# Token scales moved from the norm's input to the projections' results, and the stage boundaries of a 16-stage network re-ordered

## The reference, cut to what matters

```
norm 0 -> stick-breaking attention     norm 1 -> MLP (squared relu, 4096 hidden)
norm 2 -> retention                    norm 3 -> MLP
norm 4 = final norm of the first network, its result is the new h
norm 5 -> gated linear attention (GLA) norm 6 -> conv FFN (2816 x 2 hidden, 3 taps over tokens, silu gate)
norm 7 -> shared keys and values of NSA;  norm "7b": the same h and root, another gain -> NSA's queries
norm 8 -> conv FFN                     norm 9 -> output
rms_norm(x, g) = x * rsqrt(mean(x*x) + 1e-6) * g        one factor for each token (rstd), one gain for each column
```

## Time and profile before

| what | value |
|---|---|
| times of three runs | 1498.61, 1498.81, 1499.96 us; median 1498.81 |
| span of the profiled execution | 1498.3 us, 0.5 below the median of the runs |
| TensorE busy | 1402.6 us (94%) |
| VectorE, ScalarE, POOL busy | 829.9 (55%), 728.0 (49%), 254.1 us (17%) |
| chain that ended last | TensorE 82%, VectorE 7%, ScalarE 5%, waits for nothing shown 3%, POOL 2% |
| mean granted TensorE clock | 0.980 |
| memory read | 229 MB, 154 GB/s over the span |

### The profile page before, as it was taken

The page is one execution under the profiler, slowest core; times in us unless marked ns, Lnnn a source line. Parts: engine busy times, 40 slices in busy tenths (PEclk is TensorE's granted clock), DMA queues, the critical chain, the costliest instruction groups (busy, mean ns, idle before and its releaser), DMA issues.

```text
span 1498.3 us, 21802 instructions
## 1 busy us (share of the span) xinstructions
PE 1402.6 (94%) x8780; PEld 1241.0 (83%) x8780; DVE 829.9 (55%) x897; ACT 728.0 (49%) x896; POOL 254.1 (17%) x219
## 2 busy tenths in 40 slices
PE   6977999999999899999999889999989887999997
PEld 6956889988987688989887869999988665799996
DVE  4443655556544546555457646665656765465664
ACT  5476544444344335444447435555555465355553
POOL 0011000002500000000001303333302234043332
PEclk9999999999999999999999999999999989999999
DMA  8520555554554244555533145555544302255551
GB/s 310 174 108 1 183 193 194 192 177 164 174 193 163 90 169 157 196 196 172 193 129 138 56 146 182 183 193 184 180 137 147 111 1 84 95 187 181 185 196 56
DMA packets 32616, 231.12 MB, mean 154 GB/s; under 512 B 3616, under 2 KB 3616, under 8 KB 5408
## 3 DMA queue, kind: packets, MB, share of 16 engines
q1 hardware_dynamic: 31104, 224.41, 43.1%
q10 hardware_dynamic: 1440, 5.68, 1.0%
HBM read 229.02 MB, written 1.05 MB: 154 GB/s over the span
## 4 chain that ended last, share of the span: by engine, by line
PE 82%; DVE 7%; ACT 5%; issue 3%; POOL 2%; DMA 0%; ACTq 0%; POOLq 0%; DVEq 0%
PE ps L509 25%; PE ps L510 25%; PE ps L511 25%; DVE w_lo L1283 1%; POOL arena L468 1%; PE ps L721 1%; DVE h L1338 1%; PE ps L865 1%; ACT w_hi L939 1%; PE ps L872 1%; ACT x_hi L953 1%; ACT L1052 1%; DVE x_lo L1295 1%; POOL arena L438 1%; PE ps L495 0%
## 5 line engine op out<-in xcount | busy, mean ns | idle before, releaser
L1283 DVE TENSOR_TENSOR w_lo<-ring,w_hi 128x2048 fp32r<-128x2048 f32 x212 | 486.3, 2297 | 363.8 <-ACT w_hi L939 363.4
L939 ACT ACTIVATE w_hi<-ring 128x2048 fp32r<-128x2048 f32 x212 | 404.5, 1909 | 237.7 <-PE ps L511 236.3
L509 PE MATMUL ps<-x_hi,w_hi 128*128 128x256 f32 x1664 | 475.1, 285 | 10.2 <-DVE x_lo L1295 10.2
L510 PE MATMUL ps<-x_lo,w_hi 128*128 128x256 f32 x1664 | 474.4, 285 | 0.0
L511 PE MATMUL ps<-x_hi,w_lo 128*128 128x256 f32 x1664 | 474.3, 285 | 0.0
L509 PEld LDWEIGHTS ps<-x_hi,w_hi 128*128 128x128 f32 x1664 | 322.7, 194 | 13.1 <-issue 8.9
L510 PEld LDWEIGHTS ps<-x_lo,w_hi 128*128 128x128 f32 x1664 | 322.5, 194 | 1.2
L511 PEld LDWEIGHTS ps<-x_hi,w_lo 128*128 128x128 f32 x1664 | 322.8, 194 | 0.0
L509 PE MATMUL ps<-w_hi,y_hi 128*128 128x512 f32 (+1 forms) x624 | 244.1, 391 | 14.4 <-issue 6.2
L510 PE MATMUL ps<-w_lo,y_hi 128*128 128x512 f32 (+1 forms) x624 | 241.6, 387 | 0.0
L511 PE MATMUL ps<-w_hi,y_lo 128*128 128x512 f32 (+1 forms) x624 | 241.1, 386 | 0.0
(11 more groups left out here) (197 smaller groups left out, 1293.4 us busy)
## 6 DMA issues: line engine op xcount, KB each, us to landing
ring<-ws SPq DMA_DIRECT2D x212, 1024.0 KB, 4.9
tab<-tables ACTq DMA_DIRECT2D x4, 550.0 KB, 3.6
rowg<-rows ACTq DMA_DIRECT2D x3, 512.0 KB, 4.5
h<-x SPq DMA_DIRECT2D x2, 512.0 KB, 5.7
out<-arena SPq DMA_DIRECT2D x2, 512.0 KB, 2.6
arena<-decay ACTq DMA_DIRECT2D x1, 768.0 KB, 5.1
sm<-small ACTq DMA_DIRECT2D x1, 742.0 KB, 5.6
arena<-narrow ACTq DMA_DIRECT2D x1, 296.0 KB, 5.7
```

Source lines behind the costliest of these rows:

```text
L509: mm(o, lh, rh, start=start, stop=False, skip_group_check=True)
L510: mm(o, lh, rl, start=False, stop=False, skip_group_check=True)
L939: A(w_hi[:, s, :], ring[:, s, :], ACT.Copy).then_inc(hi_ready, 1)
L1283: V.tensor_tensor(w_lo[:, s, :], ring[:, s, :], w_hi[:, s, :].bitcast(F32), ALU.subtract).then_inc(lo_ready, 1)
```

## The change

The token factor leaves the path in front of the projections.

- **Turning over.** The unscaled `h` is transposed (`turn_over`), a token tile at a time, and `x_hi`/`x_lo` are made in tiles of 128 x 128. `keep_clock` at boundaries goes.
- **Ordering by token tile.** `close` runs the last one or two pieces of a stage for the first token tile, then for the second, with the transposes of the first tile between the second tile's matmuls.
- **Values first.** Before retention, GLA and NSA the two pieces of a `natural` projection now come first; they begin with the first token tile, and the second tile is turned over after three of their matmul groups.
- **The factor.** `fold` makes it later. Values and gates take it as ScalarE's `scale` when they are evacuated. Queries and keys take it as a product with `scale`, a 128 x 256 tile with the token factor in each row, on VectorE (`scaled`). That tile comes from two fp32 matmuls of `ones` with a diagonal (`spread`, norms 0, 2, 5 to 8). Retention's cosine and sine tables are multiplied by it. The MLPs take `1 / mean square` in the residual. In GLA `rstd4 * rstd5` is used, and the final gain is folded into norm 5's.
- **Conv FFN.** VectorE first copies each unit out of PSUM times `scale` into `conv_in`; the taps then read `conv_in` in SBUF.
- **Slots.** `ring` has 2 slots, `w_hi`/`w_lo` have 4, `y_hi`/`y_lo` 8 rows instead of 12, and up to four banks turn.

The core of the diff:

```diff
-RING = 3
+RAW = 2
+RING = 4
@@ SyncE
-                if turn is not None or g >= RING:
-                    sp.wait_ge(lo_ready, plus(g - RING + 1, turn, RING))
+                if turn is not None or g >= RAW:
+                    sp.wait_ge(lo_ready, plus(g - RAW + 1, turn, RAW))
@@ TensorE
+            def turn_over(n, t):
+                for k in range(KT):
+                    if n == 0:
+                        pe.wait_ge(x_loaded[t], 16)
+                    elif n != "7b" and k % 4 == 0:
+                        pe.wait_ge(h_ready, H_AT[4 if n == 5 else n] - 3 + 2 * t + k // 4)
+                    if t == 1 and k % 2 == 0 and n != 0:
+                        pe.wait_ge(xT_lo, 8 * XT_OF[n] + k // 2 + 1)
+                    r = nc.tensor.transpose(ps[:, 4 + k // 2, t * T + (k % 2) * P:t * T + (k % 2 + 1) * P],
+                                            h[:, t, k * P:(k + 1) * P], ident)
+            def spread(n):
+                pe.wait_ge(diag_ready, SCALE_OF[n] + 1)
+                for t in range(TT):
+                    r = mm(ps[:, 2, t * P:(t + 1) * P], ones[:, :], diag[:, t, :], start=True, stop=True, ...)
+            def close(pieces, n):
+                for t in range(TT):
+                    for i, (g, tiles) in enumerate(pieces):
+                        end = i == len(pieces) - 1
+                        for k in range(2):
+                            r = add(g, tiles, t, k, False, end)
+                            if n is not None and t == 1 and end and k == 0 and len(pieces) == 1:
+                                turn_over(n, 0)
+                        if t == 0 and end:
+                            r.then_inc(half_done, 1)
+                        if t == 1:
+                            r.then_inc(done, 1)
+                            if n is not None and not end:
+                                turn_over(n, 0)
@@ hidden.up
+                        if u == 0 and n in SCALE_OF:
+                            spread(n)
@@ NSA on TensorE
-            norm(7)
+            natural(G_NSA, (0, 1), first=7)
+            spread(7)
             for u in range(4):
-                transposed(G_NSA + u, u, nsa_freed, first=7 if u == 0 else None)
-            natural(G_NSA + 4, 4, nsa_freed)
-            pe.wait_ge(nsa_freed, 6)
-            norm("7b")
+                transposed(G_NSA + 2 + u, 4 + u)
+            for t in range(TT):
+                pe.wait_ge(nsa_kv, 4)
+                turn_over("7b", t)
@@ ScalarE
+            def norm(n, *late):
+                tiles(n, 0)
+                tiles(n, 1)
+                for g in late[:-1]:
+                    refill(g)
+                sumsq(4 if n == 5 else n)
+                refill(late[-1])
@@ ScalarE, GLA's tree
             for j in range(8):
-                if j % 2 == 0:
+                if j in (0, 2, 4):
...
                 A(w, w, ACT.Exp, scale=-1.0 / 16.0).then_inc(gla_decay, 1)
                 if j < 4:
-                    refill(G_GLA + 5 + j)
+                    refill(G_GLA + 6 + j)
@@ ScalarE, NSA
             for u in range(2):
-                act.wait_ge(done, G_NSA + u + 1)
+                act.wait_ge(nsa_kv, u + 1)
...
-                refill(G_NSA + u)
+                refill(G_NSA + 2 + u)
             for u in range(2, 4):
-                evac(u, G_NSA + u, ns_k[:, u - 2, :, :], nsa_freed)
-                refill(G_NSA + u)
...
+                refill(G_NSA + 2 + u)
             for t in range(TT):
-                evac(4 + t, G_NSA + 5, ns_v[:, t, :], nsa_freed)
-            norm_tiles("7b")
-            refill(G_NSA + 5)
+                tiles("7b", t)
@@ VectorE
+            def scaled(dst, src, sc, by=1.0):
+                return V.scalar_tensor_tensor(dst, src.rearrange("p (a t) -> p a t", t=T), by,
+                                              sc.unsqueeze(1).broadcast_to([P, 2, T]), ALU.mult, ALU.mult)
@@ VectorE, residual
+                        if n in (2, 4):
+                            r = V.scalar_tensor_tensor(v, ps[:, 2 * t + c, :], rfold[:, t:t + 1], v, ALU.mult, ALU.add)
+                        else:
+                            r = V.tensor_tensor(v, ps[:, 2 * t + c, :], v, ALU.add)
+                        r.then_inc(h_ready, 1)
+                    if following is not None:
+                        tiles(following, t)
@@ VectorE, ffn
+                        dve.wait_ge(done, plus(g + 1, turn, st.each))
+                        scaled(conv_in[:, u % 2, :, :], ps[:, bank(u), :], scale).then_inc(freed, 1)
+                        dve.wait_ge(freed, plus(u + 1, turn, st.units))
+                        dve.wait_ge(base, plus(u + 1, turn, st.units))
                         for e in range(2):
                             v = conv[:, u % 2, e, 1:T]
-                            V.scalar_tensor_tensor(v, ps[:, bank(u), e * T:(e + 1) * T - 1], par(u, 2 + e, turn), v,
+                            V.scalar_tensor_tensor(v, conv_in[:, u % 2, e, 0:T - 1], par(u, 2 + e, turn), v,
                                                    ALU.mult, ALU.add).then_inc(tap, 1)
@@ VectorE, NSA
+            for u in range(4):
+                dve.wait_ge(done, G_NSA + 2 + u + 1)
+                scaled(ns_kvs[:, u, :, :] if u < 2 else ns_k[:, u - 2, :, :], ps[:, 4 + u, :], scale).then_inc(nsa_kv, 1)
+                refill(G_NSA + 2 + u)
+            for t in range(TT):
+                tiles("7b", t)
```

More of the change, by code:

```diff
@@ L511, in mm3, with transposed @@
                 return mm(o, ll, rh, start=False, stop=stop, skip_group_check=True)
[L513 removed]
+            def transposed(g, b, first=None, turn=None, each=0):
                 split(g, turn, each)
[L516 to L517 removed]
                 s = g % RING
@@ new lines, in hidden @@
+            def hidden(n, st, freed, ready, following):
+                def up(c, turn):
+                    for u in (2 * c, 2 * c + 1):
+                        if turn is not None or u >= 6:
+                            pe.wait_ge(freed, plus(u - 3, turn, st.units))
+                        transposed(st.up(c) + u % 2, bank(u), first=n if u == 0 else None, turn=turn, each=st.each)
+                        if u == 0 and n in SCALE_OF:
+                            spread(n)
+                def down(c, turn):
+                    pe.wait_ge(ready, plus(2 * c + 2, turn, st.units))
+                    if c == 0 and n in SCALE_OF:
+                        pe.wait_ge(scale_ready, SCALE_OF[n] + 1)
+                    pieces = [(st.down(c) + i, (4 * (c % 2) + 2 * i, 4 * (c % 2) + 2 * i + 1)) for i in range(st.dn)]
+                    if c == st.chunks - 1:
+                        close(pieces, following)
+                    else:
+                        for i, (g, tiles) in enumerate(pieces):
+                            accumulate(g, tiles, c == 0 and i == 0, turn, st.each)
@@ L1191, in _ @@
+            for u in range(4):
+                refill(G_NSA + 6 + u)
+                if u == 0:
                     for i in range(2):
@@ L1254, in _ @@
                     .then_inc(nsa_oT_hi, 1)
-            for i in range(3):
+            for i in range(2):
                 refill(G_NSA + 14 + i)
-            norm(8, G_NSA + 17)
+            norm(8, G_NSA + 16, G_NSA + 17)
+            spread(8, scale)
             ffn(1)
@@ L1584, in _ @@
                  .then_inc(nsa_blocks, 1)
-            for g in range(7, 10):
-                refill(G_NSA + g)
+            for u in range(4):
+                dve.wait_ge(done, G_NSA + 6 + u + 1)
+                scaled(ns_q[:, 2 * u:2 * u + 2, :], ps[:, 4 + u, :], scale, 0.125).then_inc(nsa_q_in, 1)
+                refill(G_NSA + 6 + u)
             dve.wait_ge(nsa_blocks, 2)
```

682 lines of the change are left out of this document (397 added, 285 removed).

## The result

The changed kernel takes 1504.73 us (median of 8 runs, 1501.84 to 1507.45), the kernel before 1499.53 us in the same sets (8 runs, 1498.61 to 1500.82). The ratio is 1.0032 with a 95% interval of 1.0023 to 1.0042: slower by 0.3%, where 1.1% faster was forecast. The profiled execution is the slowest of the eight (1507.45 us, span 1505.6), 2.7 above the median, so the spans differ by 7.4 us where the medians differ by 5.2: some 2 us of what the profiles show belong to this one execution.

A forecast was written before the change was run, and what follows sets the result against it. TensorE, busy 94% of the 1498.3 us span, was taken as the bound, so only its waits could be won. Terms 5.1 + 3.95 + 1.5 + 2.55 + 7.4 - 2.4 - 1.7 = 16.4 gave 1482.5 us, range 1471 to 1496.

The forecast's parts named there:

- the one on the conv FFNs: Conv FFN chunks: VectorE-ScalarE cycle of 16.8 to 16.95 us against TensorE's 16.95, no mid-stage stall; -1.7 us (0 to -10).
- Rival B: Conv FFNs: VectorE becomes the bound, cycle 17.3 us, 7 to 14 us lost, 1489 to 1497 us; chance 15%.
- rival C: Conv FFNs: taps, now reading only SBUF, wait for POOL's `y_lo`; 32 us delay less cover, 1511 us, slower; chance 8%.
- My sign of a wrong prediction: Conv FFNs: the prediction is wrong if, among other signs, the taps' mean is over 0.4 us.
- the 1.20 us in front of the first scores: NSA: of the 1.20 us the first scores waited for VectorE, 1.1 was to go.
- the term "0": Kernel start: first matmul 0.5 us earlier, spread costs 0.55; net 0 (-1 to 1).
- The 0.5 around the span: Whole kernel: 0.5 us between the 1498.3 us span and the 1498.8 us median, added to the forecast span.
- the wait of the spread for the diagonal: Conv FFN starts (boundaries 6 and 8): spread behind the first unit waits for the diagonal; 1.25 us given back each.
- "7b": Norm inside NSA: tiles stand behind the next refill in both queues; stall 11.5 us instead of 4.7, -6.8.
- the clock I had booked half: Boundaries 3, 6 and 8: slow stretches costing 5.1 us may vanish; half, 2.55 us, taken (0 to 5.1).
- Rival D: All boundaries: without warming matmuls the clock falls at every one, five more slow stretches at 1.7 us; 1491 us; chance 8%.
- Rival A: NSA: the queue in front of "7b" does not bite, the -6.8 and -1.7 are gone; 1474 us; chance 15%.

The follow-up runs named there:

- e1: Changed kernel without VectorE's scaled copy in the conv FFNs; ScalarE's base and VectorE's taps read PSUM as before, token factor left out of the hidden units: 1486.48 us.
- e6: Changed kernel with the conv FFN's scaled copy made twice, the first into a buffer nobody reads: 1525.47 us.
- e2: Changed kernel, same instructions, with a weight remainder on VectorE between a conv FFN unit's scaled copy and its taps: 1488.35 us, ratio to before 0.9924.
- e9: Changed kernel with e2's order in the conv FFNs and e4's NSA order and start warming, GLA as the change left it: 1477.96 us, ratio 0.9855.
- e10: As e9, with the conv FFN's product of silu and value made by VectorE behind the taps for every unit: 1478.14 us, ratio 0.9857.
- e5: The kernel before the change with no warming matmuls at its boundaries, nothing else: 1504.3 us, one run.
- e4: Changed kernel: NSA splits before raw copies, 7b tiles before last refill; GLA's last gates and ScalarE refill behind the tree; six warming products at the start: 1502.45 us.
- e7: Changed kernel with e2's, e4's and e8's GLA orders; last chunk's up refills behind taps, last unit's product on VectorE: 1488.01 us, ratio 0.9921.
- e8: Changed kernel with GLA's refill moved on both ScalarE and VectorE, and in NSA only norm 7b's tiles before the last refill: 1508.7 us.

## Why the prediction was wrong

**The step that failed** is the one on the conv FFNs: "the handing back and forth with ScalarE closes a cycle that I put at 16.8 to 16.95". It is 17.7, measured, and its price 8.7 and 9.2 us more than forecast, 17.9 of 23.8. Rival B (15%) had the cycle as the mechanism, with 17.3 and 7 to 14 us in all; the real figure is beyond its end, so the range ended too early. B's own sum, 21 times 0.35, is 7.4 us before the cover, and the 14 at its upper end has no working; 21 times the measured 0.77 is 16. Nor is VectorE full, as B's title has it (busy 65.6 of 102 us). I summed what each engine does and added a guess for the hand-offs, in place of walking one chunk instruction by instruction. From start to start in the rows above: copy, base and first unit's taps 4.0 (974.61 to 978.59), remainder 2.2, copy, base and second unit's taps 4.2 (980.79 to 984.95), silu 0.6, product *at its held price, which the earlier trace rows showed*, 2.3 (the second remainder runs beside it), `y_hi` 0.3, `w_hi` 1.9, remainder 2.2: 17.7. e1, e6 and e2 show the copy and its place in the order as the cause. I also placed the danger of VectorE and POOL holding one another wrongly: rival C had the taps wait for `y_lo`, but in the changed kernel they average 481 ns against 478 in e1; what is held is POOL's product, and it was held before too (mean 2295 ns), when TensorE set the pace. My sign of a wrong prediction, a mean of the taps over 0.4 us, says nothing: it was 478 ns before the change already.

**Mis-sized in the rest:** at NSA the head came as forecast (47.2 for 47.0 up to the small projection). From there to the first score it is 49.0 us where it was 47.2: I had let 1.1 of the 1.20 us in front of the first scores go, and 4.4 stand there now (row L961 above). From the first score to the stage's end it is 112.8 us where it was 107.7; tile 0's transposes are 1.1 of that, and about 4 are the scores, whose code is not changed. Windows of 108 us from the first score on, and the first 2 us of them, before and after:

```profile
1187.00:1295.00 108.00, 92.57 (x531) 70.19 (x532) 59.46 (x117) 54.88 (x163) 32.27 (x32) 0.94 0.15 49
...
1187.00:1189.00 2.00, 1.55 (x8) 1.12 (x8) 0.29 (x1) 0.56 (x1) 0.00 (x0) 1.00 0.02 8
```

```profile
1182.00:1290.00 108.00, 93.52 (x512) 69.90 (x513) 59.25 (x116) 54.96 (x162) 32.23 (x32) 0.88 0.13 43
...
1182.00:1184.00 2.00, 1.64 (x6) 1.49 (x7) 0.21 (x1) 0.74 (x1) 0.00 (x0) 0.50 0.19 70
```

The mean granted clock (last but two in a row) is 0.94 and 0.88 in the same work: 2 x 0.06 x 108 = 13 and 2 x 0.12 x 108 = 26 us at the lower level of 1.2 GHz. Part of it is chance of the execution: e9 and e10 have the same NSA code and 0.88 and 0.94 here, with NSA at 201.8 and 198.0. But part goes with the change. The two traces with the NSA of the kernel before (before, e5) wait 1.2 us in front of the first score and run it at full clock, with 0.94 and 0.95 in the 108 us; all ten traces on the changed kernel wait 4.1 to 4.6 us there and start the scores at half clock, for 3.4 to 10.2 us, and six of the ten have 0.88. That the longer wait is what brings the slow stretch is not shown, since no run shortened it; so how much of the 4 us the change costs stays open. At the start the term "0" was +2.1: TensorE's first matmul comes at 16.15 instead of 15.16. ScalarE now loads a table (1.28 us) and writes four `x_hi` in front of the first `w_hi`, which starts at 11.84 instead of 9.99, and the first remainder at 13.80 instead of 11.94. The slow stretch behind it, which was there before too, is 20 matmuls long instead of some 14; it varies from run to run. The 0.5 around the span was wrong as well: it compared the span of one execution with the median of others, while every run on record lies 1.7 to 2.3 above its own span.

**Right:** the boundaries (2.83 for 3.05), retention, GLA (copies 85.8 us behind the close, forecast 86.3), the wait of the spread for the diagonal (0.97 for 1.25), "7b" (11.8 for 11.5). Of the clock I had booked half; all three stretches were saved, where half was a guess and the better end luck. Rival D is false: no boundary fell. Rival A did not come by itself, but e4 shows what it took: 8.6 us up to the first score, where A has 8.5. My remark that an earlier evacuation would give GLA 2 to 6 us is untested: e4, e7 and e8 moved the last evacuation later, behind the tree.

## What to carry to other kernels

If a second engine no longer reads a result itself but a first engine's copy of it, it waits for the first engine's queue from then on. Walk one whole period through all queues, with hand-offs and held durations, and compare it with the bound to a per cent, since 4% over ten chunks shows only at the end of the stage. An engine with a third of idle time can be the bound by order alone; move independent work into the wait before adding buffers or moving work. A refill that is moved on one engine must be moved on all, and with few slots it takes its transfer with it.

## What was not expected of the hardware

The clock did not fall behind gaps of 2.8 us that hold transposes, with no warming in them (boundaries 1, 3, 6 and 8). In the kernel before it fell behind four boundaries of seven, all 6.7 us long and with warming matmuls in them, and not behind boundary 5, 11.0 us long with 6.17 us of warming; in e5, without any, it fell behind five of seven and still not behind boundary 5, where TensorE had 7.0 us of idle and then 3.35 us of transposes. In the NSA scores the same instructions had 13 to 26 us at half clock from one execution to the next. At the start of the kernel before, the spacing of the matmuls (0.21 us) is that of half clock while the window reads 1.00: where the two differ, the spacing is the time that is paid.
